# A state space layer's input product: from fp32 matmuls to three fp32r passes, with its convolution's first tap on ScalarE

## The reference, cut to what matters

```
h    = rmsnorm(x, mix_norm)                       # 256 x 1024
proj = h @ ssd_w_in                               # 1024 x 8256: z | conv channels | dt
conv = silu(depthwise_conv(proj[conv channels], ssd_conv_w, 5 taps) + ssd_conv_b)   # 6144 channels
x_h, B_f, B_b, C_f, C_b = split(conv)             # 2048, and 4 x 1024
dt   = softplus(proj[dt] + dt_bias)
y    = scan forward(x_h, dt, B_f, C_f) + scan backward(x_h, dt, B_b, C_b) + d * x_h
y    = rmsnorm(y * silu(z), ssd_norm)
x    = x + y @ ssd_w_out
```

## Time and profile before

| | us |
|---|---|
| median of 3 runs | 3259.15 |
| lowest and highest of them | 3258.29, 3270.25 |
| the profiled execution's own time | 3268.64 |
| its span in the trace | 3266.9 |
| ssd stage, first quarter's start to the last instruction of the stage's product | 1997.7 to 2268.5 |

### The profile page before, as it was taken

How to read it: one execution, slowest core, us unless ns; L and a number is a source line. 1 busy time by engine, 2 the same in 40 slices (tenths; PEclk the granted TensorE clock), 3 DMA queues, 4 the chain that set the end, 5 groups by cost and what they waited for, 6 DMA issues and landing times.

```text
span 3266.9 us, 42153 instructions
## 1 busy us (share of the span) xinstructions
PE 3011.1 (92%) x16936; PEld 2591.8 (79%) x16937; DVE 1827.4 (56%) x2130; ACT 1272.2 (39%) x1314; POOL 299.5 (9%) x228
## 2 busy tenths in 40 slices
PE   5979998887999999999998999999999899798998
PEld 4857996366777777777886998887899899676998
DVE  6475434955787778778554453883244344143552
ACT  1223331005666667666443431343143333123441
POOL 1006902930000000000000000012000000000000
PEclk7959999898999999999998999999999999899999
DMA  7844564045999899889553554443355456631462
GB/s 250 264 148 145 186 218 123 1 131 165 309 324 300 292 332 317 283 292 341 181 193 113 167 184 130 129 129 103 103 183 177 134 180 193 137 108 52 155 203 71
DMA packets 572649, 608.12 MB, mean 186 GB/s; under 512 B 37385, under 2 KB 520812, under 8 KB 572524
## 3 DMA queue, kind: packets, MB, share of 16 engines
q1 hardware_dynamic: 558720, 602.37, 56.7%
q10 hardware_dynamic: 13804, 3.94, 0.8%
HBM read 605.22 MB, written 1.05 MB: 186 GB/s over the span
## 4 chain that ended last, share of the span: by engine, by line
PE 80%; DVE 7%; DMA 5%; issue 3%; ACT 2%; POOL 2%; ACTq 1%; SPq 0%; DVEq 0%; POOLq 0%
PE bank L1038 24%; PE bank L905 9%; PE bank L1458 7%; PE bank L931 4%; PE bank L1359 3%; PE bank L1352 2%; PE bank L1388 2%; PE bank L1389 2%; PE bank L1356 2%; PE bank L1393 2%; DMA ring<-in_o_exp_up 2%; DMA ring<-in_o_exp_down 2%; PE bank L917 2%; PE bank L1013 1%; PE bank L1009 1%
## 5 line engine op out<-in xcount | busy, mean ns | idle before, releaser
L2325 DVE TENSOR_TENSOR ring_r<-ring,store_area_r 128x2048 fp32r<-128x2048 f32 (+1 forms) x318 | 746.4, 2376 | 168.3 <-ACT store_area_r L1712 165.6
L1712 ACT ACTIVATE store_area_r<-ring 128x2048 fp32r<-128x2048 f32 (+1 forms) x318 | 618.9, 1975 | 191.2 <-PE bank L1038 79.2
L2688 DVE TENSOR_TENSOR ring_r<-ring,store_area_r 128x3072 fp32r<-128x3072 f32 x64 | 195.1, 3089 | 78.6 <-ACT store_area_r L2010 78.6
L1458 PE MATMUL bank<-hT,ring 128*128 128x256 f32 x1024 | 230.0, 380 | 0.0
L1038 PE MATMUL bank<-sq_r,store_area_r 128*128 128x256 f32 x1408 | 206.5, 290 | 20.9 <-ACT sq_r L1748 20.9
L905 PE MATMUL bank<-hT,ring 128*128 128x256 f32 x896 | 200.1, 385 | 26.0 <-DVE hT L2208 22.4
L905 PEld LDWEIGHTS bank<-hT,ring 128*128 128x128 f32 x896 | 172.5, 193 | 51.2 <-issue 27.2
L1458 PEld LDWEIGHTS bank<-hT,ring 128*128 128x128 f32 x1024 | 190.8, 190 | 27.1 <-issue 3.1
L1038 PEld LDWEIGHTS bank<-sq_r,store_area_r 128*128 128x128 f32 x1408 | 187.1, 195 | 25.2 <-issue 22.4
L1038 PE MATMUL bank<-sq_r,ring_r 128*128 128x256 f32 x1408 | 200.8, 286 | 0.0
L1038 PE MATMUL bank<-hT_r,store_area_r 128*128 128x256 f32 x1408 | 199.4, 285 | 0.0
(11 more groups left out here) (431 smaller groups left out, 5128.4 us busy)
## 6 DMA issues: line engine op xcount, KB each, us to landing
ring<-in_o_exp_gate SPq DMA_DIRECT2D x88, 1024.0 KB, 6.2
ring<-in_o_exp_up SPq DMA_DIRECT2D x88, 1024.0 KB, 8.8
ring<-in_ffn_w_gu SPq DMA_DIRECT2D x88, 1024.0 KB, 7.5
ring<-in_o_exp_down SPq DMA_DIRECT2D x32, 1536.0 KB, 8.1
ring<-in_ffn_w_down SPq DMA_DIRECT2D x32, 1408.0 KB, 8.8
ring<-in_o_exp_down SPq DMA_DIRECT2D x32, 1280.0 KB, 10.9
ring<-in_ssd_w_in SPq DMA_DIRECT2D x32, 1024.0 KB, 7.1
ring<-in_e_mod_mix_w SPq DMA_DIRECT2D x12, 1024.0 KB, 9.4
```

Source lines behind the costliest of these rows:

```text
L1458: ins = mm(dense_bank(i, s)[:, half * T:(half + 1) * T], slot(u, s, KD)[:, k, half * P:(half + 1) * P], h(k), start=(k == 0), stop=(k == K ...
L1712: activation(dst, slot(u, s, kk), ACT.Copy).then_inc(w_high, 1)
L2325: nc.vector.tensor_tensor(slot(u, s, kk, rounded=True), slot(u, s, kk), as_f(high), ALU.subtract).then_inc(w_low, 1)
L2688: vec.tensor_tensor(down_wide(u, rounded=True)[:, j:j + m, :], down_wide(u)[:, j:j + m, :], as_f(down_high_wide(i)[:, j:j + m, :]), ALU.su ...
```

## The change

- The 64 quarters run in three fp32r passes of eight matmuls each, as the feed-forward stages do: high weights x high h, low weights x high h, high weights x low h. The dt columns stay as they were.
- ACT makes the high parts (`high_parts`), DVE the low parts (`low_parts`). There is one place for the high parts of s = 0 and one for s = 1. So ACT makes those of unit i + 1, s = 0, at t = 4i + 2, behind `high_used` (PE has done quarter 4i + 1), and those of s = 1 at t = 4i + 4, behind `unit_done` of unit i, ahead of `unit_out`. The first unit's two are made inside the norm, between the squares and the root. The high part of h is eight copies on ACT, its low part eight subtractions on DVE; those overwrite hT and wait for the dt columns' matmuls.
- The convolution's first tap moves to ACT: four Identity activations 128x256 with scale and bias from SBUF, behind `unit_out`, counted in `tap_ready`. DVE does taps 1 to 4, one per quarter, 16 instructions a unit; part 0 waits for `tap_ready`.
- DVE makes the low part of s = 1 at t % 4 == 1 and that of the next unit's s = 0 at t % 4 == 3, both ahead of its taps.

```diff
 quarter(t), PE:
+                    out, cols = dense_bank(i, s)[:, half * T:(half + 1) * T], slice(half * P, (half + 1) * P)
                     if half == 0:
-                        pe.wait_ge(slot_full[2 * u.r + s], u.full())
+                        pe.wait_ge(ssd_high, 2 * i + s + 1)
                     for k in range(KD):
-                        ins = mm(dense_bank(i, s)[:, half * T:(half + 1) * T], slot(u, s, KD)[:, k, half * P:(half + 1) * P], h(k),
-                                 start=(k == 0), stop=(k == KD - 1))
-                    if s == half == 1:
-                        ins.then_inc(unit_done, 1)
+                        if t == 0:
+                            pe.wait_ge(h_high, parts_before("ssd_in") + k + 1)
+                        mm(out, ssd_high_block(s, k, cols), ssd_h_high(k), start=(k == 0), stop=False)
+                    if half == 0:
+                        pe.wait_ge(ssd_low, 2 * i + s + 1)
+                    for k in range(KD):
+                        mm(out, slot(u, s, KD, rounded=True)[:, k, cols], ssd_h_high(k), start=False, stop=False)
+                    for k in range(KD):
+                        if t == 0:
+                            pe.wait_ge(h_low, parts_before("ssd_in") + k + 1)
+                        ins = mm(out, ssd_high_block(s, k, cols), h_lo[:, k, :], start=False, stop=(k == KD - 1))
+                    if half == 1:
+                        ins.then_inc(unit_done if s else high_used, 1)
...
 ssd(), ACT:
+                def high_parts(i, s):
+                    u = Unit(first + 1 + i)
+                    se.wait_ge(slot_full[2 * u.r + s], u.full())
+                    for rows, high in ssd_high_parts(s):
+                        ins = activation(high, ssd_slot(u, s, rows), ACT.Copy)
+                    ins.then_inc(ssd_high, 1)
+
+                norm("mix_0", meanwhile=lambda: [high_parts(0, s) for s in range(2)])
+                for k in range(KD):
+                    se.wait_ge(h_ready, KD * H_BEFORE["mix_0"] + k + 1)
+                    activation(ssd_h_high(k), hT[:, k, :], ACT.Copy).then_inc(h_high, 1)
...
                     ins.then_inc(evac, 1)
+                    se.wait_ge(evac, first + 1 + i + 1)
+                    for n, j in enumerate(conv_tiles(i)):
+                        ins = activation(arena[:, j * T:(j + 1) * T], conv_buf[:, n, 0:T], ACT.Identity, bias=vcol("ssd_conv_b_2", j),
+                                         scale=conv_col(0, j))
+                    ins.then_inc(tap_ready, 1)
...
-                for t in range(4, QUARTERS + 1):
+                for t in range(2, QUARTERS + 1):
                     for g, step in scan_steps(t):
                         scan(g, step)
+                    if t % 4 == 2 and t < QUARTERS - 4:
+                        se.wait_ge(high_used, EVEN_USED + t // 4 + 1)
+                        high_parts(t // 4 + 1, 0)
                     if t % 4 == 0:
                         i = t // 4 - 1
+                        if t < QUARTERS:
+                            se.wait_ge(unit_done, Unit(first + 1 + i).at(1))
+                            high_parts(i + 1, 1)
                         unit_out(i)
...
 ssd(), DVE:
+                low_parts(0, 0)
+                ve.wait_ge(unit_done, Unit(first).at(1))
+                for k in range(KD):
+                    ve.wait_ge(h_high, parts_before("ssd_in") + k + 1)
+                    vec.tensor_tensor(h_lo[:, k, :], hT[:, k, :], as_f(ssd_h_high(k)), ALU.subtract).then_inc(h_low, 1)
+                low_parts(0, 1)
...
+                    if t % 4 == 1 and t > 1:
+                        low_parts(t // 4, 1)
+                    if t % 4 == 3 and t < QUARTERS - 4:
+                        low_parts(t // 4 + 1, 0)
                     i, part = t // 4 - 1, t % 4
-                    if SSD_UNITS[i][0] == "conv":
+                    if i >= 0 and SSD_UNITS[i][0] == "conv":
                         taps(i, part)
```

58 lines of the change are left out of this document (39 added, 19 removed).

## The result

| | before | changed |
|---|---|---|
| median, us (9 runs each) | 3264.24 | 3280.21 |
| lowest and highest | 3256.15, 3270.25 | 3273.39, 3291.93 |
| profiled execution | 3268.64 | 3280.03 |
| its span, mean granted clock | 3266.9, 0.951 | 3278.3, 0.955 |

The ratio of the times is 1.0054, 95% interval 1.0037 to 1.0071: slower, by 16 us. The forecast was 3277, the range 3246 to 3293, and slower by over 0.5% its likeliest class. The forecast stood on a median of 3259.15 from three executions; the nine above have 3264.24, to which +18 would have given 3282.

What follows compares the result with a forecast made beforehand. PE bounded the kernel before; a cycle through DVE and ACT would replace it. +3.1 - 1.2 + 6.4 + 11.4 - 5.2 = +14.5, with +2 handing over and +1.5 clock +18 us: median 3277, range 3246 to 3293.

Steps and rivals of the forecast that it cites:

- a ring of DVE and ACT: Conv units without scan steps: a cycle through DVE and ACT replaces PE as bound, 0.6 us longer than PE's was.
- start: Before quarter 0: ACT's first high parts between squares and root make the root 3.1 us later.
- quarters 16 to 27: First twelve quarters with scan steps, without L2829 and output products for group 0: 57.2 us against 50.8, +6.4.
- quarter 52 to the end: Gate units, no taps: PE's work 47.2 us plus about 2 of waits, 49.1 against 54.3, a gain of 5.2.
- PE's pace: All 64 quarters: eight fp32r matmuls take 0.96 us, a quarter 2.88, so 38.4 us less over 64.
- The plain cycle: Conv units without scan steps, quarters 0 to 15: one cycle from low part to low part takes 14.5 us.
- The loaded quarters 28 to 39: Twelve quarters with scan steps: DVE's work 50.0, GpSimd 3.5, waits 6.6, sum 60 us against 54.3 before.
- The clock: PE's waits once per unit bring spells of half clock, mostly hidden by DVE's chain: +1.5 us, bounds 0 and 22.
- The wait at L1521: Quarters with scan steps: step 1's product waits for conv_out, which stands behind the first taps; 1.1 us.
- GpSimd: Twelve quarters with scan steps: one of two POOL multiplications hits DVE's taps, 3.5 us, bounds 0 and 7.
- Rival 2: Conv units: DVE's work alone is the bound if waits for tap_ready vanish; 3248 us; chance 0.18.
- Rival 1: Conv units: the whole gain arrives if low parts land before PE's second pass; 35 us less, 3224; chance 0.08.

Runs made afterwards that it cites:

- e1: The changed kernel with DVE's low part of s = 1 made ahead of tap 1's wait for ACT: 3268.11 us, 1.0015 of the kernel before.
- e3: The changed kernel with all five taps back on DVE, three passes kept: 3275.64 us, 1.0038 of the kernel before.
- e5: The changed kernel with ACT doing three of a unit's four first taps a second time, unread: 3301.39 us, 1.0131 of the kernel before.
- e14: The changed kernel with PE repeating the first pass four extra times before the scan steps of quarters 29 and 41: 3272.05 us, 1.0038 of the kernel before.
- e6: The changed kernel with GpSimd multiplying only 16 of 1536 columns of each group's backward weights: 3275.5 us, 1.0045 of the kernel before.
- e11: The changed kernel with four order edits: low part before tap 1, first high parts after root, high parts before scan steps, conv_out before unit_out: 3260.7 us, 0.9993.

## Why the prediction was right, and where its terms were off

The forecast of the class, the size and the mechanism held: a ring of DVE and ACT replaced PE as the bound, PE's waits stood at the second pass and were ended by DVE's low part, and tap 1 waited for ACT (e1, e3 and e5). Of its other signs, the quarters of the stage took 284.5 us, not under 270, and GpSimd's multiplications at 2102.31, 2163.18 and 2224.28 stand 60.9 and 61.1 us apart. That the sum came within 1 us is in part luck, since terms that were off cancel. Term by term:

| term | predicted | measured |
|---|---|---|
| start | +3.1 | +3.4 |
| quarters 0 to 15 | -1.2 | 0.0 |
| quarters 16 to 27 | +6.4 | +3.9 |
| quarters 28 to 51 | +11.4 | +14.8 |
| quarter 52 to the end | -5.2 | -5.0 |
| handing over, and the clock | +2 and +1.5 | within the pieces above |
| sum | +18 | +17.1 |

- **PE's pace** of 0.96 per pass held to the hundredth. PE's busy time fell by 30.5 us and not by 38.4; from the norm's sum on PE lost 12.5 us to the half clock, against 1.7 before.
- **The plain cycle** was put at 14.5 us and came 14.42 apart the first time, 15.70 the second, with a spell of half clock in between. (The prediction's own terms add up to 8.97 for its 9.1, and to 54.6 for its 54.9, so its gain would be 1.5; there was none.) Four first taps took 2.08 us, not 1.8. The estimate of 2.0 that the prediction worked out from the Trainium skill (ScalarE: Activation LUTs, "What ACT_TABLE_LOAD costs") was nearer. In the groups by shape one tap takes 591 ns, against 475 with one such operand, from PSUM; the 116 between them are more than the 93 of the Trainium skill, but the inputs differ:

```profile
L2100 ACT ACTIVATE store_area<-silu_g,vc 128x256 f32<-128x256 f32 x48 | 24.9, 591 | 0.4
```

- **Quarters 16 to 27** were 57.2 less 50.8 in the prediction, and are 55.5 less 51.6. Even the 51.6 of the kernel before was in its trace and was not read from it; the 57.2 does not follow from the terms given (60 less 2 x 0.87 is 58.3).
- **The loaded quarters 28 to 39** came to 60 us by two errors that nearly cancel. DVE's work with GpSimd's hold was put at 53.5 us and is 50.62. Most of that is the taps: four begin and give way to the next instruction in 1.58 us (2124.63 to 2126.21 on DVE's timeline), 0.395 each, where I had divided a row's length by its count, 0.437, which counts the last one's tail once per row. The waits were put at 0.4, 1.7, 3.4 and 1.1, together 6.6, and are 0.75, 2.02, 5.06 and 2.41, together 10.24. That the next twelve took 62.5 and not 60.9 was not foreseen either.
- **The clock** is the term that was sized wrong. "Mostly DVE's chain hides that", +1.5: e14 gives 4.5 us for two spells alone, so the chain does not hide it. The bound of 22 held. The fault was to ask which engine is busiest; in a ring each engine's part is on the path in its turn, so slow matmuls count wherever the ring passes PE.
- **The wait at L1521** was named but priced at 1.1 us of DVE's time, where DVE waits 2.41; PE itself stands idle for 4.74, and this wait is what brings the clock down (e14). ACT's silu stands behind a table load there, the copies and the first taps.
- **GpSimd**: 3.5 us were added to every twelve quarters; e6 shows 0.1, 2.2 and 1.2. One of the two in twelve quarters hit taps and one fell into a wait, as predicted; but it was counted in full. The trace of the changed kernel also shows DVE holding GpSimd: the multiplication that began at 2071.78 took 4.72 us, where the next five took 3.46 to 3.52, and a two-input multiplication of DVE had begun at 2071.39. The prediction set the Trainium skill (SBUF — State Buffer, "Who interferes with whom") against the rows of before, which showed no such delay; the trace of the changed kernel agrees with the Trainium skill in both directions.
- **Rival 2**, DVE's work as the bound, had 53.5 us for twelve loaded quarters; e11 has 54.4 and 55.0. It comes near the mended kernel, not this one. Its 3248 was too low: e11's median is 3260.7, with waits of PE for DVE's scan steps that I had not counted. Rival 1 needed the low part 2.4 us earlier in plain units: e1 gave it that, and the plain quarters then took 47.3 us, 8.8 less; the loaded ones from quarter 28 on gave 2.7 and 4.1 and stayed above those of the kernel before.

What stays open: how much of e5's last 6 us is the clock, and what an order without the 4 us of waits that e11 leaves on DVE would give.

## What to carry to other kernels

Splitting fp32 products into fp32r passes buys PE time with DVE and ACT time, so do it unit by unit, only where DVE's stretch has room for the subtraction; here 7 of 16 units, in the mended order, were a gain of 14 us, all 16 in that order no gain, and all 16 as they were written a loss of 16. Before giving an engine with slack a part of another's work, follow the semaphores around: if the new step closes a ring, its latency counts, in e5 all of it, however idle the engine is, and the first thing to try is to place the instruction that the next engine waits for ahead of the wait. In a ring, a stretch of half clock on PE counts as well, even where PE is not the busiest engine.

## What the runs showed of the hardware that was not expected

An idle time of PE of 2.25 us before 2016.69 was followed by a granted clock of 1.00, one of 1.93 us before 2031.11 by 0.50 two microseconds later (steps of 1 us, PE):

```profile
2017.00:2018.00 1.00, 1.00 (x11) 1.00 0.00 0
```
```profile
2033.00:2034.00 1.00, 1.00 (x7) 0.50 0.00 0
```

So within one stage the length of a wait alone does not tell whether the clock falls. And 3.84 us of matmuls that nothing needs, in each of two waits of 4.74 us, made the stage 4.7 us shorter.
